# First mixer: 128 tokens against 128 keys, and the decay levels of the gated branch copied two at a time

## The reference, cut to what matters

```python
# selected attention (4 heads of 128)
limit = (c + 1) * CHUNK                       # CHUNK = 64
score = jnp.where((key_pos < limit)[None, None, :], score, -jnp.inf)
_, idx = lax.top_k(score, topk)               # topk = 64
s = jnp.where(valid[:, :, None, :], s, -jnp.inf)
p = jax.nn.softmax(s, axis=-1)
out = jnp.einsum('bthk,btkhd->bthd', p.astype(v.dtype), vs)
# gated linear attention (4 heads, 64 channels, values of 128)
decay = jnp.exp(jnp.where(causal[:, :, None], diff, -jnp.inf))
att = jnp.einsum('bhtd,bhsd,bhtsd->bhts', qc, kc, decay)
o = o_inter + jnp.einsum('bhts,bhse->bhte', att, vc)
```

## Time and profile before

| | |
|---|---|
| median of 3 runs | 978.67 us (978.29, 978.67 and one of 1363.52) |
| profiled execution | 978.44 us, span 976.6 us |
| TensorE matmul | busy 966.8 us, 99% of the span |
| VectorE | busy 619.5 us, 63% |
| ScalarE | busy 549.2 us, 56% |
| GpSimd | busy 130.3 us, 13% |
| granted TensorE clock | 0.999 of 2.4 GHz |
| transfers | 168.45 MB, mean 172 GB/s |

### The profile page before, as it was taken

How to read it: one execution, slowest core, us unless ns; L and a number is a source line. 1 busy time by engine, 2 the same in 40 slices (tenths; PEclk the granted TensorE clock), 3 DMA queues, 4 the chain that set the end, 5 groups by cost and what they waited for, 6 DMA issues and landing times.

```text
span 976.6 us, 14013 instructions
## 1 busy us (share of the span) xinstructions
PE 966.8 (99%) x5786; PEld 854.3 (87%) x5786; DVE 619.5 (63%) x911; ACT 549.2 (56%) x782; POOL 130.3 (13%) x44
## 2 busy tenths in 40 slices
PE   9999999999999999999999999999999999999997
PEld 7888888888888788888888888899999999999886
DVE  5997957777322566747877322376547689888643
ACT  7676346666433567847766433544444688666442
POOL 0021041000665000011000656300000000000000
PEclk9999999999999999999999999999999999999999
DMA  8553224555555543344555555464443525555441
GB/s 295 224 193 147 87 87 176 198 188 177 194 189 200 188 172 130 130 147 187 187 180 206 176 178 210 143 216 152 154 169 131 215 103 209 189 189 196 176 170 44
DMA packets 25091, 168.45 MB, mean 172 GB/s; under 512 B 2813, under 2 KB 3508, under 8 KB 5188
## 3 DMA queue, kind: packets, MB, share of 16 engines
q1 hardware_dynamic: 24740, 167.22, 47.2%
q10 hardware_dynamic: 288, 0.33, 0.1%
HBM read 166.49 MB, written 1.05 MB: 172 GB/s over the span
## 4 chain that ended last, share of the span: by engine, by line
PE 97%; DVE 1%; ACT 1%; DMA 1%; issue 0%; SPq 0%; DVEq 0%; ACTq 0%
PE bank L675 23%; PE bank L676 23%; PE bank L677 23%; PE bank L757 12%; PE bank L761 6%; PE bank L929 2%; PE bank L703 1%; DMA raw<-w_stream 1%; PE bank L897 0%; PE bank L946 0%; PE bank L814 0%; PE bank L1014 0%; PE bank L1142 0%; ACT whi L1229 0%; PE bank L818 0%
## 5 line engine op out<-in xcount | busy, mean ns | idle before, releaser
L1835 DVE TENSOR_TENSOR wlo<-raw,whi 128x2048 fp32r<-128x2048 f32 (+2 forms) x152 | 310.6, 2044 | 262.3 <-ACT whi L1229 262.3
L1229 ACT ACTIVATE whi<-raw 128x2048 fp32r<-128x2048 f32 (+1 forms) x154 | 293.0, 1904 | 151.5 <-PE bank L677 149.9
L2547 POOL TENSOR_TENSOR wlo<-raw,whi 128x1024 fp32r<-128x1024 f32 (+1 forms) x37 | 129.1, 3492 | 491.7 <-ACT whi L1229 484.3
L757 PE MATMUL bank<-nhl,whi 128*128 128x512 f32 x512 | 130.3, 395 | 0.0
L675 PE MATMUL bank<-mhi,whi 128*128 128x258 f32 x384 | 108.7, 283 | 0.0
L757 PEld LDWEIGHTS bank<-nhl,whi 128*128 128x128 f32 x512 | 92.1, 189 | 18.6 <-DVE nhl L1848 1.6
L676 PE MATMUL bank<-mlo,whi 128*128 128x258 f32 x384 | 108.3, 282 | 0.0
L677 PE MATMUL bank<-mhi,wlo 128*128 128x258 f32 x384 | 108.2, 282 | 0.0
L675 PE MATMUL bank<-nhl,whi 128*128 128x258 f32 (+3 forms) x320 | 92.9, 290 | 0.0
L676 PE MATMUL bank<-nhl,whi 128*128 128x258 f32 (+3 forms) x320 | 91.3, 285 | 0.0
L677 PE MATMUL bank<-nhl,wlo 128*128 128x258 f32 (+3 forms) x320 | 90.5, 283 | 0.0
(11 more groups left out here) (314 smaller groups left out, 1767.3 us busy)
## 6 DMA issues: line engine op xcount, KB each, us to landing
raw<-w_stream SPq DMA_DIRECT2D x154, 1024.0 KB, 4.8
cst<-consts SPq DMA_DIRECT2D x1, 1088.0 KB, 6.9
h<-x_rows SPq DMA_DIRECT2D x4, 256.0 KB, 5.4
raw<-w_stream SPq DMA_DIRECT2D x2, 512.0 KB, 6.4
out_rows<-e SPq DMA_DIRECT2D x3, 256.0 KB, 2.0
e<-g_post SPq DMA_DIRECT2D x1, 512.0 KB, 3.5
raw<-w_stream SPq DMA_DIRECT2D x1, 352.0 KB, 9.3
b<-consts_x SPq DMA_DIRECT2D x1, 272.0 KB
```

Source lines behind the costliest of these rows:

```text
L757: return pe.matmul(us[c].t[:, :], w[:, k, c * P:c * P + P].hi, nboth[:, k, :], start=k == 0, stop=k == 7)
L1229: act.activation(whi[j][:, 0:n], raw[j][:, 0:n], ACT.Copy).then_inc(s_hi.up(i))
L1835: dve.tensor_tensor(wlo[j][:, 0:m], raw[j][:, 0:m], whi[j][:, 0:m].bitcast(F32), ALU.subtract).then_inc(s_lod.up(i))
L2547: pool.tensor_tensor(wlo[j][:, m:n], raw[j][:, m:n], whi[j][:, m:n].bitcast(F32), ALU.subtract).then_inc(s_lop.up(i))
```

## The change

What it does:

- The scores of the first 128 tokens are made against the first 128 keys alone. A head then has 384 columns instead of 512: `SEL`, the sum, the exponential and the division have 384. The maximum is taken by two instructions (128 and 256 columns) instead of one, and the division is made by two `tensor_scalar` with a scalar per token instead of one `tensor_tensor` with a spread operand. GpSimd's write of the fourth square goes.
- The 8 predicated copies of a block become 4 of 128x256, each taking two neighbouring levels of one bank into the two halves of `am`. All four write the same 256 columns, so each waits until the one before it has finished.
- VectorE then adds the two halves of `am` (a new `tensor_tensor`, 128x128) into one of two buffers in the space that the narrower scores left free, and raises a new semaphore `s_am`.
- `gla_2` on TensorE makes one product with the values instead of two. It waits for `s_am` where it waited for both banks to be released.

```diff
-                on.wait_ge(*use["gl", n, 0].gone())
-                on.wait_ge(*use["gl", n, 1].gone())
-                for i in range(2):
-                    x = pe.matmul(oo, am[:, i * P:i * P + P], VB[:, tt, hd * P:hd * P + P], start=i == 0, stop=i == 1 and tt == 0)
+                on.wait_ge(*s_am.at(n))
+                x = pe.matmul(oo, AMS[n % 2], VB[:, tt, hd * P:hd * P + P], start=True, stop=tt == 0)
...
-                    x = pe.matmul(u.t[:, tt * 256:tt * 256 + 256], QKT[:, hd, tt * P:tt * P + P], QKT[:, 4 + hd, :], start=True, stop=True)
+                    x = pe.matmul(u.t[:, KEYS_OF[tt]], QKT[:, hd, tt * P:tt * P + P], QKT[:, 4 + hd, 0:P * (tt + 1)], start=True, stop=True)
...
-                for i in range(4):
-                    for half in range(2):
-                        if i == 0:
-                            on.wait_ge(*us[half].done())
-                        else:
-                            on.wait_ge(own.sem, own.n - 1)
-                        x = dve.copy_predicated(am[:, half * P:half * P + P], gm[:, (half * 4 + i) * P:(half * 4 + i + 1) * P],
-                                                us[half].t[:, i * P:i * P + P])
-                        x.then_inc(own.up() if i < 3 else us[half].free)
-                        if i == 2 and half == 1:
+                for half in range(2):
+                    on.wait_ge(*us[half].done())
+                    if half:
+                        on.wait_ge(*us[0].gone())
+                    for i in (0, 2):
+                        if i:
                             on.wait_ge(*own.last())
+                        c = i * P
+                        x = dve.copy_predicated(am.rearrange("p (l t) -> p l t", l=2),
+                                                gm[:, half * 512 + c:half * 512 + c + 256].rearrange("p (l t) -> p l t", l=2),
+                                                us[half].t[:, c:c + 256].rearrange("p (l t) -> p l t", l=2))
+                        x.then_inc(us[half].free if i else own.up())
+                on.wait_ge(*us[1].gone())
+                dve.tensor_tensor(AMS[n % 2], am[:, 0:P], am[:, P:256], ALU.add).then_inc(s_am.up(n))
...
-                dve.tensor_tensor(y, u.t[:, :], SEL, ALU.add).then_inc(u.free)
+                dve.tensor_tensor(y, u.t[:, 0:3 * P], SEL, ALU.add).then_inc(u.free)
                 on.wait_ge(*u.gone())
-                dve.tensor_reduce(mx, y.rearrange("p (t n) -> p t n", t=2), AX.X, ALU.max).then_inc(own.up())
+                for tt in range(2):
+                    dve.tensor_reduce(mx[:, tt:tt + 1], y[:, KEYS_OF[tt]], AX.X, ALU.max).then_inc(own.up())
...
-                dve.tensor_tensor(yv, yv, bc(sm.rearrange("p (t o) -> p t o", o=1), [P, 2, 256]), ALU.mult).then_inc(s_pn.up(hd))
+                for tt in range(2):
+                    y = SSH[hd % 2][:, KEYS_OF[tt]]
+                    dve.tensor_scalar(y, y, sm[:, tt:tt + 1], None, ALU.mult).then_inc(s_pn.up(hd, tt))
```

More of the change, by code:

```diff
@@ L516, in block_kernel @@
         SC = A(512).rearrange("p (t n) -> p t n", t=2)
-        SEL = A(512)
-        SELv = SEL.rearrange("p (t n) -> p t n", t=2)
+        SEL = A(3 * P)
         QKT = A(2048).rearrange("p (k t) -> p k t", k=8)
@@ L525, in block_kernel @@
         DE = A(512)
-        SS = A(1024).rearrange("p (j n) -> p j n", j=2)
+        SS = A(1024)
         PT = A(768).rearrange("p (j n) -> p j n", j=2)
@@ L531, in block_kernel @@
         DEs = [DE, A(512)]
-        RT = SS.rearrange("p j n -> p (j n)")
+        RT = SS
+        KEYS_OF = (slice(0, P), slice(P, 3 * P))
+        SSH = [SS[:, j * 3 * P:(j + 1) * 3 * P] for j in range(2)]
+        AMS = [SS[:, (6 + j) * P:(7 + j) * P] for j in range(2)]
         GL = A(256)
@@ L630, in block_kernel @@
         s_qrs, s_qg = sig("qrs", grid(2, 2)), sig("qg", grid(2, 2))
-        s_am0, s_sel0, s_sel, s_ropea = sig("am0", [0]), sig("sel0", [0]), sig("sel", range(2)), sig("ropea", range(2))
+        s_am0, s_am, s_sel, s_ropea = sig("am0", [0]), sig("am", range(8)), sig("sel", range(2)), sig("ropea", range(2))
         s_sig, s_og = sig("sig", range(2)), sig("og", range(2))
         s_ynsq, s_obss, s_obrs, s_yn, s_obhi = (sig(n, range(2)) for n in ("ynsq", "obss", "obrs", "yn", "obhi"))
-        s_nmx, s_prob, s_pn = sig("nmx", range(4)), sig("prob", grid(4, 2)), sig("pn", range(4))
+        s_nmx, s_prob, s_pn = sig("nmx", range(4)), sig("prob", grid(4, 2)), sig("pn", grid(4, 2))
         s_cathi = sig("cathi", [(0, hd) for hd in range(4)] + [(1, hd) for hd in range(8)])
@@ L938, in gla_2 @@
                 u = begin("ob", tt) if hd == 0 else use["ob", tt]
-                am = AM[:, n % 2 * 256:n % 2 * 256 + 256]
                 oo = u.t[:, hd * P:hd * P + P]
@@ L964, in att_1 @@
                 for tt in range(2):
-                    x = pe.matmul(u.t[:, tt * 256:tt * 256 + 256], QKT[:, hd, tt * P:tt * P + P], QKT[:, 4 + hd, :], start=True, stop=True)
+                    x = pe.matmul(u.t[:, KEYS_OF[tt]], QKT[:, hd, tt * P:tt * P + P], QKT[:, 4 + hd, 0:P * (tt + 1)], start=True, stop=True)
                 x.then_inc(u.full)
             def att_3(hd):
-                yv = SS[:, hd % 2, :].rearrange("p (t n) -> p t n", t=2)
                 u = begin("pT", hd)
-                on.wait_ge(*s_pn.at(hd))
+                on.wait_ge(*s_pn.at(hd, 1))
                 for i, (tt, kb) in enumerate(((0, 0), (1, 0), (1, 1))):
-                    x = pe.transpose(u.t[:, i * P:i * P + P], yv[:, tt, kb * P:kb * P + P], ident)
+                    x = pe.transpose(u.t[:, i * P:i * P + P], SSH[hd % 2][:, KEYS_OF[tt]][:, kb * P:kb * P + P], ident)
                 x.then_inc(u.full)
@@ L1432, in att_1 @@
                 for tt in range(2):
-                    act.activation(yv[:, tt, :], yv[:, tt, :], ACT.Exp, bias=mx[:, tt:tt + 1], scale=scale,
+                    y = SSH[hd % 2][:, KEYS_OF[tt]]
+                    act.activation(y, y, ACT.Exp, bias=mx[:, tt:tt + 1], scale=scale,
                                    accum_out=sm[:, tt:tt + 1]).then_inc(s_prob.up(hd, tt))
@@ L2011, in vector_program @@
             for tt in range(2):
-                dve.tensor_scalar(SELv[:, tt, 0:P * (tt + 1)], wks[tt], -2.0e38, BIGNEG, ALU.is_gt, ALU.mult).then_inc(s_sel.up(tt))
+                dve.tensor_scalar(SEL[:, KEYS_OF[tt]], wks[tt], -2.0e38, BIGNEG, ALU.is_gt, ALU.mult).then_inc(s_sel.up(tt))
             lo(13)
@@ L2080, in att_1 @@
                 u = use["qk", hd]
-                y = SS[:, hd % 2, :]
+                y = SSH[hd % 2]
                 mx = small[:, 128 + 2 * hd:130 + 2 * hd]
-                on.wait_ge(*s_sel0.at(0))
                 on.wait_ge(*s_sel.at(1))
@@ L2534, in gpsimd_program @@
             pool.memset(AM, 0.0).then_inc(s_am0.up(0))
-            pool.memset(SEL[:, P:256], BIGNEG).then_inc(s_sel0.up(0))
             for i in range(2, NTILE):
```

## The result

The changed kernel takes 979.96 us in the median of its runs (979.53 to 982.21) against 978.57 for the kernel before in the same comparison: ratio 1.0016, 95% interval 1.0009 to 1.0024. It is 1.4 us slower, far inside 2%, but clear of the noise. The forecast was 979.4 in a range from 975.8 to 981.5; mine was the case in which VectorE becomes the bound, priced at +0.7.

A forecast was written before the change was run, and what follows sets the result against it. VectorE was taken to become the loop's bound: its chain grows 2.9 - 1.3 - 0.5 = 1.1 us, delaying the output projection 0.7. 978.44 + 0.7 = 979.1, plus 0.2 for the median, predicted as 979.4 us, range 975.8 to 981.5.

The forecast's parts named there:

- What bounds the kernel: In the loop TensorE and VectorE are both full and equally long; after the change VectorE becomes the bound.
- TensorE has 2.8 us less to do, the ceiling of a gain: In the loop, value products save 1.8 us and score products 1.0; together 0.3% of the kernel.
- A block's copies cost VectorE more, not less: Four serial copies plus the new sum take 2.08 us a block in place of 1.72; 8 blocks +2.9 us.
- The heads save 1.3 us: On VectorE in the loop, each of four heads saves 0.33 us through shorter sum, maximum and division.
- The two waits for ScalarE are absorbed, -0.5: VectorE's two loop waits for ScalarE, 0.24 and 0.25 us, are over when VectorE comes after longer copies.
- The end of the loop: Last product starts 0.15 us after its sum, at 129.02 against 128.05; one product instead of two saves 0.22.
- The sum: VectorE's loop chain grows 1.1 us, so the output projection starts 0.7 us later and the whole execution takes 0.7 more.
- The signs: Loop trace: VectorE near 100% busy, TensorE waits of about 3 us at L945 and L971, output projection at 129.3.
- The rule against this reading: Skill rule that semaphores between VectorE ops cost nothing extra; by it four serial copies lose nothing and the change gains.
- Rival 1: Instruction count decides, not the wait: serial copies overlap at 0.34 us from start to start, giving 976.1 us; 17%.
- Rival 2, a dear copy: The 256-column copy costs 0.477 to 0.59 us in its chain, so the time ends at 981.0 to 984.5; 18%.
- Rival 3, the clock: TensorE's clock falls in its new loop gaps, each us of work at 1.2 GHz costing one more; 1%.

The follow-up runs named there:

- e7: The changed kernel with TensorE's value product made twice, the second in place of the first; 980.13 us.
- e8: The changed kernel with the second bank's copies sent to another buffer, so the four alternate, and levels 4 to 7 left out of the sum; 975.75 us.
- e5: The changed kernel's same instructions in another VectorE order, copies standing between those of the heads and norms; 976.68 us.
- e4: The changed kernel without the sum: four serial copies of 256 columns, then two value products on TensorE; 977.67 us.
- e3: The changed kernel with eight copies of 128 columns as before, then the sum of the halves and one product; 979.40 us.

## Why the prediction was right, and what was mis-sized

- *What bounds the kernel.* Right. In the changed kernel VectorE bounds the loop: e7 gives TensorE 1.8 us more to do, and the time grows by 0.2.
- *TensorE has 2.8 us less to do, the ceiling of a gain.* Right, and reached: e8 is 2.8 below the kernel before.
- *A block's copies cost VectorE more, not less.* The step and its sign are right, its size is not. I took 0.43 + 0.04 for a copy and its successor's wait; it is 0.443 + 0.052 = 0.495. A block grew by 0.46 and not 0.36 us; over 8 blocks that is 0.8 us, more than the whole miss of the forecast.
- *The heads save 1.3 us.* Nearly. From the reciprocal that begins the division to the sum it is 0.65 us now (109.11 to 109.76) against 0.80, and from the sum to the first copy 1.31 (105.60 to 106.91) against 1.52: 4 x 0.36 = 1.4.
- *The two waits for ScalarE are absorbed, -0.5.* Right in kind: no `clo` instruction of the loop has a wait now. The size is 0.7: before, such a block took 2.06 us to the `clo` instruction (114.06 to 116.12) and not 1.72, because the wait also cost the overlap with the last copy. 2 x 0.34 = 0.7; now the block takes 2.20 (115.22 to 117.42), about as the others do.

```profile
114.06 1.82 DVE L2043 COPY_PREDICATED a<-cst,bank 128x128 f32<-128x128 uint32 x8
116.12 0.43 DVE L2053 TENSOR_TENSOR clo<-bank,chi 128x256 fp32r<-128x256 f32 x1 [0.24 <-ACT chi L1399]
```

- *The end of the loop.* Product after sum: 0.15 us by L1029, here 0.06. But the product that waited takes 0.32 us to the next (129.65 to 129.97), not 0.22. These two errors cancel. VectorE's spare time before the change was 0.28 - 0.06 = 0.22 us rather than 0.13.
- *The sum.* +0.7 for a measured +1.4. With the terms as measured VectorE's chain grows by 3.7 - 1.4 - 0.7 = 1.6 us (in the traces 28.95 us, from 98.82 to 127.77, and now 30.55), less 0.22 of spare time and 0.12 of the last products: +1.3, and the loop is 1.27 longer. The block alone would have made it +1.5, and the heads and the waits take 0.3 of that back. That the time lies in the stated range says little, since the range also covers a gain of 2.8 us; what bears the prediction out is the sign and the cause.
- *The signs.* TensorE's waits were forecast at about 3 us at L945 and L971; they are 3.6 there, and no other line of the loop has one. The output projection was forecast at 129.3 and starts at 130.12, or 129.91 without the shift that was there when the loop began. VectorE "near 100%" did not come: it is busy for 93% of both stretches, because the pauses in front of waiting instructions do not count as busy.
- *The rule against this reading* (the Trainium skill, VectorE: DVE Perf Modes, The DRAIN you can't avoid): by it, a wait between neighbours costs nothing extra. Here the changed kernel and e8 have 32 copies of one size, 0.495 apart with the wait and 0.33 without. The same section also says that a next op that is not held starts earlier, which the prediction left out and which the overlap of 0.10 us agrees with. Rival 1, serial copies 0.34 apart, is refuted, and e5 shortens VectorE's chain by 3.3 us with the order alone.
- *Rival 2, a dear copy.* Refuted by its own sign (0.48 us or more): 443 ns is 11 above the 432 that the small copy and the slope give (295 + 137). *Rival 3, the clock.* Not seen; the granted clock is 1.00 through waits of up to 1.1 us.

The case for the change fails in its second half only: it saves TensorE 1.8 us and charges VectorE 3.7 in a stretch where VectorE had 0.2 to spare. e5 shows that most of the charge can be avoided with the same instructions; it stays 0.9 us above e8.

## What to carry to other kernels

Before cutting instructions of the busiest engine, look at the stretch they are in, and at the second engine's time from start to start there, not at its share of the span. Count what a merge does to the dependences: eight instructions in two alternating chains (1.72 us a block) can be cheaper than four in one (1.84 in e4). Where one engine's list holds two independent chains, deal their instructions out alternately; here that was worth 3.3 us, where the change alone lost 1.4. It pays only where that engine is the bound: the kernel before in such an order was not run, but its TensorE has no wait in the loop, so I expect nothing of it.

## What the runs showed of the hardware

- Two neighbouring VectorE instructions that do not wait for each other overlap by about 0.10 us (copies of 437 ns, 333 ns apart, e8). One that waits for its neighbour starts 0.05 us after that has ended (0.495 for 443; 0.03 for the sum behind the copies, and 0.10 in e3). So between copies a wait for one's neighbour costs 0.16 us, a third of a 256-column copy; with one other instruction between them it costs nothing (e5: 104.21, 104.54 and 104.73).
- A predicated copy from PSUM with a mask takes 295 ns at 128 columns in the kernel before, and at 256 columns 443 where each waits for its neighbour and 437 where none does (e8). Against the 437 that is 1.11 ns a column, a little above the 1.07 of the `tensor_tensor` rows.
- A `tensor_scalar` of 256 columns with a scalar per token takes 348 ns in the changed kernel, where the rows of 128 and 1024 columns had given 0.35 us, half a nanosecond a column.
